# Four of twenty-four gate tiles computed as two more pairs of block products

## The reference

```python
h = rms_norm(x, norm_g)
u = h @ w_in
v_c, b_c, c_c, z_c, q, k, v, z_a, gate_logits = split(u)
y_c = b_c * causal_depthwise_conv(c_c * v_c, conv_w) * silu(z_c)
y_a = y_c @ w_conv_out
o = sliding_window_attention(rms_norm(q), rms_norm(k), v, sinks) * silu(z_a)
y_b = o @ w_attn_out
g_a, g_b = split(sigmoid(gate_logits + gate_b))
x = x + (g_a * y_a + g_b * y_b) @ w_out
```

## Time and profile before

| what | value |
|---|---|
| median of 3 runs | 2374.72 us |
| the profiled execution, its own time | 2376.15 us |
| its span, first to last instruction | 2374.4 us |
| PE busy | 2354.4 us, 99% |
| DVE, ACT, POOL busy | 64%, 41%, 6% |

### The profile page before, as it was taken

One profiled execution on the slowest core, in us unless ns is written; L12 is line 12 of the kernel. 1 busy time (PEld: TensorE's weight loads), 2 busy tenths in 40 slices (PEclk: granted clock), 3 DMA queues, 4 the chain that ended last, 5 costly groups with the idle time before them and its releaser, 6 DMA issues.

```text
span 2374.4 us, 30564 instructions
## 1 busy us (share of the span) xinstructions
PE 2354.4 (99%) x11300; PEld 1959.9 (83%) x11300; DVE 1527.4 (64%) x2395; ACT 978.1 (41%) x1675; POOL 139.7 (6%) x189
## 2 busy tenths in 40 slices
PE   8999999999999999999999999999999999999998
PEld 6788888888888888888788888998888888888886
DVE  6658888847777744436555753473598888884335
ACT  6346565524344423232233343373355444442124
POOL 1000000000000010021000030021100000000000
PEclk9999999999999999999999999999999999999999
DMA  5112223345323253322110042372122222244323
GB/s 198 44 45 81 80 90 98 108 124 124 98 89 102 67 186 99 113 82 58 37 52 23 28 146 72 98 233 69 54 68 83 79 79 79 82 155 127 106 62 125
DMA packets 253361, 222.19 MB, mean 94 GB/s; under 512 B 7246, under 2 KB 225571, under 8 KB 252226
## 3 DMA queue, kind: packets, MB, share of 16 engines
q1 hardware_dynamic: 233920, 148.39, 20.5%
q0 software_dynamic: 15424, 56.53, 7.5%
q10 hardware_dynamic: 3906, 15.78, 2.1%
HBM read 171.39 MB, written 49.28 MB: 93 GB/s over the span
## 4 chain that ended last, share of the span: by engine, by line
PE 94%; DVE 4%; ACT 1%; DMA 1%; issue 1%; SPq 0%; ACTq 0%; DVEq 0%
PE bank L993 11%; PE bank L995 11%; PE bank L994 11%; PE bank L1589 4%; PE bank L1590 4%; PE bank L1591 4%; PE bank L1226 4%; PE bank L1227 4%; PE bank L1228 4%; PE bank L1177 4%; PE bank L1178 4%; PE bank L1176 4%; PE bank L1632 2%; PE bank L1630 2%; PE bank L1631 2%; PE bank L1400 1%
## 5 line engine op out<-in xcount | busy, mean ns | idle before, releaser
L1705 ACT ACTIVATE whi<-wraw 128x1024 fp32r<-128x1024 f32 (+2 forms) x159 | 160.6, 1010 | 483.9 <-PE bank L995 266.2
L2626 DVE TENSOR_TENSOR wlo<-wraw,whi 128x1024 fp32r<-128x1024 f32 (+1 forms) x174 | 204.3, 1174 | 117.5 <-ACT whi L1705 111.3
L1176 PE MATMUL bank<-xhi,whi 128*128 128x512 f32 x384 | 149.6, 390 | 0.0
L1178 PE MATMUL bank<-xhi,wlo 128*128 128x512 f32 x384 | 149.5, 389 | 0.0
L1177 PE MATMUL bank<-xlo,whi 128*128 128x512 f32 x384 | 149.5, 389 | 0.0
L993 PE MATMUL bank<-x2hi,whi 128*128 128x512 f32 x240 | 94.5, 394 | 0.0
L995 PE MATMUL bank<-x2hi,wlo 128*128 128x512 f32 x240 | 94.1, 392 | 0.0
L994 PE MATMUL bank<-x2lo,whi 128*128 128x512 f32 x240 | 94.0, 392 | 0.0
L1630 PE MATMUL bank<-ffn_hi,whi 128*128 128x512 f32 x240 | 93.4, 389 | 0.0
L1631 PE MATMUL bank<-ffn_lo,whi 128*128 128x512 f32 x240 | 93.4, 389 | 0.0
L1632 PE MATMUL bank<-ffn_hi,wlo 128*128 128x512 f32 x240 | 93.4, 389 | 0.0
(11 more groups left out here) (529 smaller groups left out, 6613.2 us busy)
## 6 DMA issues: line engine op xcount, KB each, us to landing
wraw<-in_w_in_dram SPq DMA_DIRECT2D x85, 512.0 KB, 3.9
wraw<-in_ffn_w_up_dram SPq DMA_DIRECT2D x44, 512.0 KB, 3.8
filler_spill<-filler POOLq DMA_DIRECT2D x24, 512.0 KB, 3.2
ffn_spill<-ffn_value SPq DMA_DIRECT2D x22, 512.0 KB, 3.4
gate<-filler_spill POOLq DMA_DIRECT2D x16, 512.0 KB, 3.9
wraw<-in_xattn_wkv_dram SPq DMA_DIRECT2D x16, 512.0 KB, 3.9
wraw<-in_ffn_w_down_dram SPq DMA_DIRECT2D x16, 512.0 KB, 3.7
ffn_raw<-ffn_spill ACTq DMA_DIRECT2D x14, 512.0 KB, 4.7
```

The costliest lines, as they stand in the source:

```text
L1176: pe.matmul(ps(m % 3), whi[slot][:, k, :], xh, start=(k == 0), stop=False)
L1178: last = pe.matmul(ps(m % 3), wlo[slot][:, k, :], xh, start=False, stop=(k == KT - 1))
L1705: act.activation(whi[slot][:, 0:n, 0:m], wraw[slot][:, 0:n, 0:m], ACT.Copy).then_inc(s_whi, 1)
L2626: dve.tensor_tensor(wlo[slot][:, 0:n, :], wraw[slot][:, 0:n, :], whi[slot][:, 0:n, :].bitcast(F32), ALU.subtract).then_inc(s_wlo, 1)
```

## The change

`FILL_TILES` replaces the pattern that said which gate tile is the j-th. Four gate tiles (the last two of each gate) leave the fillers, 20 stay: 18 among the units, 9 steps in each, and 2 in the tail. The four become `EXTRA_PAIRS`, pairs 14 and 15 at the end of the convolution's pairs. Their results are stored by `store_extra`, 1 MB for a pair, from the buffer `cu2` in which the pair lies; the copies of pair 15 into `cu2` wait until pair 14 has been stored. `fill_bank` turns the ring of three banks so that it ends as before.

```diff
-FILLERS = 24
-FILL_IN = 20
+FILL_TILES = [Z_A + n for n in range(8)] + [G_B + n for n in range(6)] + [G_A + n for n in range(6)]
+EXTRA_PAIRS = ((G_B + 6, G_B + 7), (G_A + 6, G_A + 7))
+FILLERS = len(FILL_TILES)
+FILL_IN = 18
...
-C_PAIRS = 2 * KT - C_PLAIN
+CONV_PAIRS = 2 * KT - C_PLAIN
+C_PAIRS = CONV_PAIRS + len(EXTRA_PAIRS)
...
+        def fill_bank(m):
+
+            return (m - 2 * FILLERS) % 3
...
+            def store_extra(e):
+
+                pool.wait_ge(s_c, 4 * (CONV_PAIRS + e) + 4)
+                pool.dma_start(fill_spill[:, FILLERS + 2 * e:FILLERS + 2 * e + 2, :], cu2[:, :, 2:2 + S])\
+                    .then_inc(FILLED[e], 16)
...
-                if p % 2 == 0:
+                if p > CONV_PAIRS:
+                    store_extra(p - CONV_PAIRS - 1)
+                elif p % 2 == 0:
                     store_conv(p // 2)
...
+            for e in range(len(EXTRA_PAIRS)):
+                pool.wait_ge(FILLED[e], RING + 16)
             load_gate(1)
...
-                        pe.wait_ge(s_free, 2 * T_F + m - 2)
+                        pe.wait_ge(s_free, 2 * T_F + m - (2 if m else 1))
...
             def c_copy_u3(p, q):
 
                 act.wait_ge(s_m, 7 * p + (4 if p == C_LAST else 5))
-                act.wait_ge(s_tap, 2 * p + 2 * C_PLAIN - 1)
+                if p > CONV_PAIRS:
+                    act.wait_ge(FILLED[p - CONV_PAIRS - 1], RING + 16)
+                else:
+                    act.wait_ge(s_tap, 2 * p + 2 * C_PLAIN - 1)
...
             def c11_c21(p, q):
 
                 dve.wait_ge(s_m, 7 * p + 7)
-                dve.wait_ge(s_tap, 2 * p + 2 * C_PLAIN)
+                if p > CONV_PAIRS:
+                    dve.wait_ge(FILLED[p - CONV_PAIRS - 1], RING + 16)
+                else:
+                    dve.wait_ge(s_tap, 2 * p + 2 * C_PLAIN)
```

More of the change, by code:

```diff
@@ L543, in hybrid_then_mixer_kernel @@
         conv_spill = nc.dram_tensor("conv_spill", [P, KT * S], F32).ap().rearrange("p (k s) -> p k s", k=KT)
-        fill_spill = nc.dram_tensor("filler_spill", [P, FILLERS * S], F32).ap()\
-            .rearrange("p (t s) -> p t s", t=FILLERS)
+        SPILLED = FILLERS + 2 * len(EXTRA_PAIRS)
+        spilled_at = {c: n for n, c in enumerate(FILL_TILES + [c for pair in EXTRA_PAIRS for c in pair])}
+        fill_spill = nc.dram_tensor("filler_spill", [P, SPILLED * S], F32).ap()\
+            .rearrange("p (t s) -> p t s", t=SPILLED)
         o_spill = nc.dram_tensor("o_spill", [D, S], F32).ap()
@@ L550, in hybrid_then_mixer_kernel @@
         RING = 16 * FILLERS // 4
-        BACK = (RING, RING, RING, RING, 16 * 3, 16 * KT, 16 * KT, 32 * KT)
+        BACK = (RING + 16, RING + 16, RING, RING, 16 * 3, 16 * KT, 16 * KT, 32 * KT)
         GATES, VO0 = s_vo_stored, 16 * KT
@@ L646, in _ @@
             for j in range(FILLERS):
-                load(T_F + j, (T_F + j) % 2, w1[:, :, (G_B, Z_A, G_A)[j % 3] + j // 3, :])
+                load(T_F + j, (T_F + j) % 2, w1[:, :, FILL_TILES[j], :])
             for n, c in enumerate((V_C, C_C, Z_C, B_C)):
@@ L651, in load_conv @@
             def load_conv(p, n):
-                c = ((V_C, C_C), (Z_C, B_C))[p % 2][n] + 1 + p // 2
+                if p < CONV_PAIRS:
+                    c = ((V_C, C_C), (Z_C, B_C))[p % 2][n] + 1 + p // 2
+                else:
+                    c = EXTRA_PAIRS[p - CONV_PAIRS][n]
                 slot = C1 if n else C0
@@ L888, in load_z @@
                     pool.wait_ge(s_og, n)
-                pool.dma_start(zg[:, :], fill_spill[:, 3 * n + 1, :]).then_inc(ZB, 16)
+                pool.dma_start(zg[:, :], fill_spill[:, spilled_at[Z_A + n], :]).then_inc(ZB, 16)
             def store_conv(b):
@@ L899, in load_gate @@
                     pool.wait_ge(s_free, 2 * (T_YB + n - 2) + 2)
-                i, j = n % KT, 2 if n >= KT else 0
-                pool.dma_start(gate[n % 2][:, :], fill_spill[:, 3 * i + j, :]).then_inc(GATES[n % 2], 16)
+                j = spilled_at[(G_A if n >= KT else G_B) + n % KT]
+                pool.dma_start(gate[n % 2][:, :], fill_spill[:, j, :]).then_inc(GATES[n % 2], 16)
+            def store_extra(e):
+                pool.wait_ge(s_c, 4 * (CONV_PAIRS + e) + 4)
+                pool.dma_start(fill_spill[:, FILLERS + 2 * e:FILLERS + 2 * e + 2, :], cu2[:, :, 2:2 + S])\
+                    .then_inc(FILLED[e], 16)
             pool.wait_ge(s_braw, 16)
@@ L1173, in filler @@
                         pe.wait_ge(s_wlo, t + 1)
-                        pe.wait_ge(s_free, 2 * T_F + m - 2)
+                        pe.wait_ge(s_free, 2 * T_F + m - (2 if m else 1))
                     xh, xl = (x[:, k, h * HALF:(h + 1) * HALF] for x in (xhi, xlo))
-                    pe.matmul(ps(m % 3), whi[slot][:, k, :], xh, start=(k == 0), stop=False)
-                    pe.matmul(ps(m % 3), whi[slot][:, k, :], xl, start=False, stop=False)
-                    last = pe.matmul(ps(m % 3), wlo[slot][:, k, :], xh, start=False, stop=(k == KT - 1))
+                    pe.matmul(ps(fill_bank(m)), whi[slot][:, k, :], xh, start=(k == 0), stop=False)
+                    pe.matmul(ps(fill_bank(m)), whi[slot][:, k, :], xl, start=False, stop=False)
+                    last = pe.matmul(ps(fill_bank(m)), wlo[slot][:, k, :], xh, start=False, stop=(k == KT - 1))
                     if k == KT - 1:
@@ L2044, in conv_step @@
                     c_weight_hi("a11", p + 1)
+                if 0 < p <= CONV_PAIRS:
+                    after(p + C_PLAIN - 1)
                 if p:
-                    after(p + C_PLAIN - 1)
                     c_copy_v(p, q)
@@ L2094, in _ @@
                 conv_step(p, p % 2)
-            after(2 * KT - 1)
             def gate_tanh(n):
@@ L2855, in filler_out @@
                     dve.wait_ge(FILLED[j % 4], 16 * (j // 4))
-                evac(T_F + j, h, 0, fill[j % 4][:, h * HALF:(h + 1) * HALF], bank_at=m % 3).then_inc(s_free, 1)
+                evac(T_F + j, h, 0, fill[j % 4][:, h * HALF:(h + 1) * HALF], bank_at=fill_bank(m)).then_inc(s_free, 1)
             def splits_due(u, early):
@@ L3080, in conv_step @@
                     c_weight_lo("a11", p + 1)
-                after_first(n)
+                if p <= CONV_PAIRS:
+                    after_first(n)
                 if not last:
                     c_weight_sum("s1", p + 1)
-                after_second(n)
+                if p <= CONV_PAIRS:
+                    after_second(n)
                 if last:
@@ L3147, in _ @@
             normed_hi(C_LAST)
-            after_first(2 * KT - 1)
-            after_second(2 * KT - 1)
             def merge(n, h):
```

## The result

The changed kernel takes 2384.55 us (median of 6 runs, 2383.72 to 2385.76) against 2374.69 us for the kernel before beside it: ratio 1.0039, 95% interval 1.0028 to 1.0049. It is slower by some 9.9 us. The forecast was 2381.8 with a range of 2377.5 to 2387.5. The profiled execution took 2384.71 us, its span is 2383.0, 8.6 more than before.

A forecast was written before the change was run, and what follows sets the result against it. PE was taken to bound the kernel, busy 2354.4 of 2374.4 us. -5.44 + 1.5 + 9.65 + 1.4 = +7.1 us gave 2381.8 us, with a range of 2377.5 to 2387.5 (8 times in 10).

The forecast's parts named there:

- The work: PE's matmuls: four plain gate tiles less, two pairs more, 24 matmuls fewer in all: -5.44 us.
- The first wait: After attention's last `weigh`, PE waits for `s_od`, the last output's sum on DVE: +1.5 us.
- The second wait: Before T_X's second half, PE waits for the last gate tile's evacuation, behind `c_forms(0)` and x: +9.65 us (8.0 to 13.2).
- The clock: Behind the second wait, PE's clock has fallen and matmuls run at half rate: +1.4 us (nothing to 2.7).
- The covers at nothing: Attention's shorter units and the last pair's copy, waiting for pair 14's store, stay hidden: no time added.

The follow-up runs named there:

- e2: Kernel after, with last gate tile's and T_X's evacuations and both splits before the forms, PE waiting for `s_od` one tile later: 2373.96 us, ratio 0.9992.
- e3: Kernel after with FILL_IN 16 for 18: extra pairs kept, four gate tiles in the tail; 2370.50 us, ratio 0.9975; run again 2370.70 us, 0.9977.
- e1: Kernel after with the last gate tile's two evacuations and the split of T_X+1 moved before `c_forms(0)`: 2378.99 us, ratio 1.0014.
- e5: Kernel after with 42 unused matmuls on PE between the two halves of T_X, filling the wait: 2382.78 us, ratio 1.0029.
- e6: Kernel after with FILL_IN 17 for 18: three gate tiles in the tail, one behind the last `weigh`: 2374.55 us, ratio 0.9995.

## Why the prediction was right

The mechanism, its two waits and their places are those on record, and so is the releaser of the long one; for the short one it follows from e2. By its steps:

- **The work, -5.44 us:** measured as -5.7 by the spans of e3 and before, and as 0.9975 and 0.9977 by the ratios (-5.9 and -5.5 us). The extra pairs are as long as the others. Pair 14 ends on DVE 19.04 us after pair 13 (below), as in the earlier trace rows. In the last pair the products come in another order, so its end on DVE says less; but PE's 16 pairs take 304.8 us from the first matmul (528.54) to the next product (833.33), 19.05 each.

```profile
798.89 1.22 DVE L3067 TENSOR_TENSOR conv_u<-conv_u,R 128x1024 f32<-128x1024 f32 x1
...
817.93 1.23 DVE L3067 TENSOR_TENSOR conv_u<-conv_u,R 128x1024 f32<-128x1024 f32 x1
```

- **The first wait, +1.5:** 1.6.
- **The second wait, +9.65:** 10.2, inside 8.0 to 13.2. The read of x went as I chose (4.8; I took 4.75): without a gate store beside it, it is faster than the 5.6 of the earlier trace rows, and with one beside it again it took 5.6 in e1. For the store I had misread the row: the 4.9 us that I shortened by 0.8 are the median over four, and the two stores that count took 3.9 before, so the fastest of the 16 (3.3) was nearly reached already, and the lower bound of 8.0 asked the store for a gain of 1.6 us that no run here shows. From their issue to that of the read of x it was 5.46 us before (494.09 to 499.55) and is 5.01 now (472.37 to 477.38): 0.45 gained of the 0.8. The rest of the missing 0.6 us is some 0.1 each in the read, in the forms (4.82 us) and in the hand-overs.
- **The clock, +1.4:** the mis-sized term. It is 2.6 us, near the upper bound of 2.7. I took the 3.0 us that dense matmuls stood at half rate in the program's start; here the rate came back only 5.3 us after PE had gone on (487.82 to 493.1). The other end, counted from the start's first transposes, came nearer. The Trainium skill's rule ("TensorE: Matmul & The Clock Gate", section "HAM oscillation - how this bites in real kernels") that a wait on a DMA between matmuls lets the array restart at half rate agrees with this case: it did so behind the wait in the kernel after, and not in e5, where PE was kept busy.
- **The covers at nothing:** held. No wait of PE in attention or in the last pair is among its waits. The 1 MB store of pair 14 was issued at 819.45 and took 5.4 us (I took 5.2); ACT's copy behind it ended at 825.96, and the product that needs it starts at 827.88, which leaves 1.9 us where I had 2.5.

The sum was 7.1, the trace shows 9.0: 1.2 of the difference is the clock, 0.6 the second wait, 0.1 the first. By the medians it is 9.9, since the profiled run of the kernel before lay 1.4 us above its median and that of the kernel after did not. All three errors point the same way and the time lies 2.75 us above the forecast; that it is inside the range is owed to the range's width as well.

The Trainium skill's formula for a transfer ("DMA: Bandwidth & Descriptors", section "Anatomy of one DMA - SWDGE (gpsimd) path") can now be laid beside two sizes of one line: 2.6 us for 128 KB and 4.8 for 512 KB. From these a fixed part of 1.9 us is estimated, near its 2, but the rest goes at some 180 GB/s and not at its 436. So its 3.2 us for the read of x were 1.6 too few. Most of what else its 6.6 us for the wait lack lies in the stretch of the two stores: 5.0 us, where the estimate by its formula leaves 3.2.

## What to carry to other kernels

Work that is taken off a bound engine is gained only if nothing used it as cover: before counting the matmuls, follow what runs on the other engines behind the piece that goes, to its end, and compare that length (here some 18 us from the last `weigh`) with what the engine still has to do. An evacuation that stands behind a wait for a transfer holds up whoever needs its bank, and taking one such wait away shows the next (T_X+1, T_X+2, the second pair's weights); here it was simpler, and faster than all reorderings that were tried, to leave the cover in its place and to take the work from where there was slack (e3). And an idle time of the matrix engine that is long enough for its clock to fall has to be priced with the slow matmuls that follow it, here a quarter on top.

## What the runs showed of the hardware

PE's clock also falls where PE is not idle. In every one of these kernels, before too, it goes to half once near the middle of the program, behind eight matmuls that use 64 and 32 rows of the array, drawn without a gap. PE's timeline of the kernel after (start, us, instruction):

```profile
1178.12 0.50 PE L1326 MATMUL bank<-gate_low_parts,gk_w_lo 32*128 32x512 f32 x1
...
1179.42 0.63 PE L1015 MATMUL bank<-x2hi,whi 128*128 128x512 f32 x1
1179.85 0.63 PE L1016 MATMUL bank<-x2lo,whi 128*128 128x512 f32 x1
...
1182.98 0.40 PE L1015 MATMUL bank<-x2hi,whi 128*128 128x512 f32 x1
```

From 1179.42 on the matmuls stand 0.43 us apart, and at 1182.98 they are at full rate again; the granted clock is 1.00 from 1178 to 1179 and 0.50 from 1180 to 1182. The nine matmuls between the two times took 1.5 us more than at the full rate. In e6 this stretch lasted 1.5 us longer than in e3. What in those eight matmuls brings the fall is not shown. Runs of one kernel spread by more than that (2374.4 to 2378.2 for the kernel before), so part of that scatter may come from here; this was not tried.
